# Two-layer diffusion backbone on one core: the first FFN in three parts instead of two, more chunks of the second FFN by the block product, and own buffers for a pair of attention's output projection

## What is computed

```python
def swiglu(h, w_in, w_out):
    gate, up = jnp.split(h @ w_in, 2, axis=-1)          # D_FF = 2816 = 22 chunks of 128
    return (jax.nn.silu(gate) * up) @ w_out

def ffn_half_step(xs, md, k, g, w_in, w_out):
    h = modulate(xs, g, md[3 * k], md[3 * k + 1])
    return xs + 0.5 * md[3 * k + 2] * swiglu(h, w_in, w_out)

mod_l = silu(c) @ ada_w[i] + ada_b[i]                   # 9 vectors of 1024 per layer
mod_c = silu(c_ctx) @ ada_w[i] + ada_b[i]
xl = ffn(xl); xl = xl + mod_l[5] * mixer(xl, xc); xl = ffn(xl)     # the same for xc, but for the last layer's end
```

## Time and profile before

| | us |
|---|---|
| median of 3 runs | 2492.06 (2489.99 to 2493.7) |
| the profiled execution, its own time | 2490.07 |
| its span | 2488.3 |
| PE busy | 2443.8 (98% of the span) |
| DVE, ACT, POOL busy | 1652.9, 916.8, 435.7 |

### The profile page before, as it was taken

The page is one execution under the profiler, slowest core; times in us unless marked ns, Lnnn a source line. Parts: engine busy times, 40 slices in busy tenths (PEclk is TensorE's granted clock), DMA queues, the critical chain, the costliest instruction groups (busy, mean ns, idle before and its releaser), DMA issues.

```text
span 2488.3 us, 40985 instructions
## 1 busy us (share of the span) xinstructions
PE 2443.8 (98%) x14665; PEld 2183.7 (88%) x14665; DVE 1652.9 (66%) x2610; ACT 916.8 (37%) x1455; POOL 435.7 (18%) x530
## 2 busy tenths in 40 slices
PE   8999999999999999999999999999999999999999
PEld 7888888888888888999899999999899988888887
DVE  6888678864888857757684747485877775643332
ACT  4333223332633322424441424243555563331221
POOL 0111111212211111000200000002666762000000
PEclk9999999999999999999999999999999999999999
DMA  7545444541155542222212222223111112433332
GB/s 237 164 144 164 131 135 139 156 120 41 46 158 155 155 129 79 66 68 63 73 52 72 72 59 84 61 68 94 26 51 44 32 34 68 127 99 95 93 107 87
DMA packets 367438, 239.51 MB, mean 96 GB/s; under 512 B 8081, under 2 KB 366066, under 8 KB 367346
## 3 DMA queue, kind: packets, MB, share of 16 engines
q1 hardware_dynamic: 366896, 238.12, 33.0%
q10 hardware_dynamic: 450, 0.18, 0.0%
HBM read 236.18 MB, written 2.10 MB: 96 GB/s over the span
## 4 chain that ended last, share of the span: by engine, by line
PE 77%; issue 13%; DVE 5%; POOL 3%; ACT 2%; DMA 0%; POOLq 0%; ACTq 0%; SPq 0%; DVEq 0%
PE pu L1495 46%; PE pu L1692 15%; PE pv L1882 5%; PE pu L1900 1%; PE pu L1537 1%; POOL ada_acc L859 1%; DVE xn L2489 1%; DVE h_lo L2496 1%; PE pu L1919 1%; PE pv L1910 1%; PE pu L1562 1%; PE pv L1789 1%; PE pv L1537 1%; PE pv L1613 0%; DVE w_lo L2138 0%
## 5 line engine op out<-in xcount | busy, mean ns | idle before, releaser
L1495 PE MATMUL pu<-h_hi,w_hi 128*128 128x512 f32 (+1 forms) x1536 | 443.9, 351 | 1.6 <-DVE w_lo L2138 1.0
L1495 PE MATMUL pu<-h_lo,w_hi 128*128 128x512 f32 (+1 forms) x1536 | 442.6, 350 | 0.0
L1495 PE MATMUL pu<-h_hi,w_lo 128*128 128x512 f32 (+1 forms) x1536 | 441.0, 349 | 0.0
L2138 DVE TENSOR_TENSOR w_lo<-w_raw,w_hi 128x1024 fp32r<-128x1024 f32 (+3 forms) x208 | 277.6, 1337 | 173.3 <-ACT w_hi L937 166.8
L937 ACT ACTIVATE w_hi<-w_raw 128x1024 fp32r<-128x1024 f32 (+3 forms) x208 | 221.0, 1063 | 443.2 <-PE pu L1495 406.9
L2165 DVE SCALAR_TENSOR_TENSOR ada_acc<-ada_raw,cs,ada_acc 128x384 f32<-128x384 f32 x602 | 345.2, 615 | 11.2 <-DVE ada_acc L2165 2.0
L1495 PEld LDWEIGHTS pu<-h_hi,w_hi 128*128 128x128 f32 x1536 | 246.7, 188 | 42.8 <-DVE w_lo L2138 2.0
L1495 PEld LDWEIGHTS pu<-h_hi,w_lo 128*128 128x128 f32 x1536 | 248.1, 188 | 40.5
L859 POOL TENSOR_TENSOR ada_acc<-ada_acc,ada_parts 128x768 f32<-128x768 f32 x86 | 147.5, 1716 | 770.2 <-ACT ada_parts L944 715.4
L1495 PEld LDWEIGHTS pu<-h_lo,w_hi 128*128 128x128 f32 x1536 | 247.2, 188 | 38.8
L2389 DVE SCALAR_TENSOR_TENSOR xT<-pu,gate,xT 128x512 f32 (+3 forms) x142 | 84.3, 630 | 289.5 <-PE pu L1495 286.3
(11 more groups left out here) (313 smaller groups left out, 4989.7 us busy)
## 6 DMA issues: line engine op xcount, KB each, us to landing
ada_raw<-in_ada_w SPq DMA_DIRECT2D x86, 768.0 KB, 4.7
w_raw<-in_ffn_w_in SPq DMA_DIRECT2D x116, 512.0 KB, 3.9
w_raw<-in_ffn_w_out SPq DMA_DIRECT2D x40, 704.0 KB, 4.5
w_raw<-in_ffn_w_in SPq DMA_DIRECT2D x108, 256.0 KB, 3.0
w_raw<-in_diff_w_qkv SPq DMA_DIRECT2D x21, 512.0 KB, 5.2
w_raw<-in_ffn_w_out SPq DMA_DIRECT2D x24, 384.0 KB, 3.3
first_raw<-in_ada_w SPq DMA_DIRECT2D x8, 1024.0 KB, 10.5
w_raw<-in_ffn_w_out SPq DMA_DIRECT2D x24, 320.0 KB, 3.3
```

The source lines that it names most:

```text
L1495: last = pe.matmul(banks(ch, s_), w[:, j, :], r[:, SEG[s_]], start=(j == 0 and i == 0), stop=(j == k - 1 and i == 2))
L2138: dve.tensor_tensor(w_lo[:, ch, 0:k * P], w_raw[:, ch, 0:k * P], w_hi[:, ch, 0:k * P].bitcast(F32), ALU.subtract).then_inc(split_ready[ch], 1)
```

## The change

**FFN 0** runs in parts of 8, 7 and 7 chunks instead of 11 and 11. It has the same matmuls of in and out units, four more out pairs (34 pairs instead of 30), and out units with K = 8 or 7 instead of 11; its tail has K = 7. **Granules:** four of layer 1 move from FFN 1 to FFN 0: `ADA_L1` is (11, 11, 0, 2), so that pairs 1 to 30 of FFN 0 and 1 to 11 of FFN 1 have a granule (before: 1 to 26, and 1 to 15). **FFN 1** runs one plain part of 7 chunks instead of 11, and then block parts; four more chunks go by the block product, in a block part of their own with K = 4 out pairs. **First block chunk:** ACT makes the SiLU and the held copy of product P5 ahead of the hi copies for the next chunk. **Attention's output:** the second pair has its own slots (a half in the upper third of `w_raw`, `w_hi`, `w_lo`; the other half in `second_raw`, `w_again`, `second_rest`, which lie over memory that the heads have left) and its own banks, and PE works on it between the steps of the last head. The core of the diff:

```diff
-PART_PAIRS = FP + OUT_PAIRS
-FFN_PAIRS = PARTS * PART_PAIRS
+FFN_PARTS = {0: ((0, 8), (8, 7), (15, 7)), 1: ((0, 7),), 3: ((0, FP), (FP, FP))}
+FFN_PAIRS = {k: sum(kp + OUT_PAIRS for _, kp in parts) for k, parts in FFN_PARTS.items()}
...
-BLK_PARTS = {1: ((11, 6, 3, 0), (17, 5, 0, 3)),
+BLK_PARTS = {1: ((7, 6, 3, 0), (13, 4, 0, 3), (17, 5, 0, 7)),
...
-ADA_L1 = (7, 15, 0, 2)
+ADA_L1 = (11, 11, 0, 2)
...
+            for ch in range(2):
+                load_unit(ch, PAIR_WO, wslot(w_raw, ch, DC), wo[:, :, ch, :])
+            sp.wait_ge(tq_done, 3 * HEADS)
+            sp.wait_ge(ss_ready, TT * HEADS)
+            for ch in range(2):
+                for b, dst in enumerate((w_raw[:, ch, DC * P:], second_raw[:, ch, :])):
+                    sp.dma_start(dst.rearrange("p (k c) -> p k c", k=DC // 2),
+                                 wo[:, b * DC // 2:(b + 1) * DC // 2, 2 + ch, :]).then_inc(second_in[ch], 16)
...
-                if nxt is None:
+                if sums:
                     block_w_hi(g + 1, P1)
+                    block_silu(g, 0)
+                    block_hold(g, 1, pu[:, 2], P5)
                     block_w_hi(g + 1, P6)
+                    block_w_hi(g + 1, P2)
...
-                k, x_hi, x_lo = FP, a_hi, a_lo
+                k, x_hi, x_lo = FFN_PARTS[0][-1][1], a_hi, a_lo
...
-            out_chunk(HEADS - 2, (0,))
+            second_out(0)
             out_sums(HEADS - 1)
+            second_out(1)
             out_spread(HEADS - 1)
-            out_chunk(HEADS - 1, (0,))
-            for j in (HEADS - 2, HEADS - 1):
-                out_chunk(j, (1,))
+            second_out(2)
+            second_out(3)
             for ch in range(2):
-                unit(ch, PAIR_WO + 1, DC, lambda j: h_hi[:, j], lambda j: h_lo[:, j], NL)
+                for j in (HEADS - 2, HEADS - 1):
+                    out_chunk(j, (ch,))
+            for j in range(4, DC):
+                second_out(j)
             wide_pe(5)
```

More of the change, by code:

```diff
@@ L93, with parts_of @@
 SUM_LAG = 2
+def parts_of(k):
+    return [(q, f0, kp, f0 + OUT_PAIRS * q, k not in BLKS and f0 + kp == FC) for q, (f0, kp) in enumerate(FFN_PARTS[k])]
 def beside(k, pair, lag=1):
@@ L140, in build @@
         KMAX = 12
+        again = ExitStack()
+        w_again = sb("w_again", [P, 2, KMAX * P], F32R, again)
+        again.close()
         w_raw = sb("w_raw", [P, 2, KMAX * P])
@@ L246, in build @@
         attn.close()
+        second = ExitStack()
+        second_skip = sb("second_skip", [P, SECOND_SKIP], F32, second)
+        second_raw = sb("second_raw", [P, 2, DC // 2 * P], F32, second)
+        second.close()
+        rest = ExitStack()
+        rest_skip = sb("rest_skip", [P, SECOND_SKIP], F32, rest)
+        second_rest = sb("second_rest", [P, 2, DC // 2 * P], F32R, rest)
+        rest.close()
         wo_late = ExitStack()
@@ L398, in build @@
         next_in = [sem(f"next_in{i}") for i in range(2)]
+        second_in = [sem(f"second_in{i}") for i in range(2)]
+        second_hi = sem("second_hi")
+        second_split = sem("second_split")
         head_in = sem("head_in")
@@ L1108, in ffn_act @@
                     else:
-                        out_pair(OUT_PAIRS - 1, nxt if last else DC, [beside(k, p0 + PART_PAIRS - 1, lag) for lag in (1, SUM_LAG)])
+                        out_pair(OUT_PAIRS - 1, nxt if last else DC, [beside(k, p0 + kp + OUT_PAIRS - 1, lag) for lag in (1, SUM_LAG)])
+                if k in BLKS:
+                    block_act(k)
             def block_w_hi(g, p, free=None):
@@ L1358, in out_hi, with second_w_out @@
                 act.activation(h_hi[:, g, 0:NL], oT[:, g, :], ACT.Copy).then_inc(onh_ready, 1)
+            def second_w_out(b):
+                for ch in range(2):
+                    act.wait_ge(second_in[ch], 32)
+                    if b == 0:
+                        act.wait_ge(qkv_done, TT * HEADS)
+                    else:
+                        act.wait_ge(second_split, 2)
+                    act.activation(second_w(ch, b)[1], second_w(ch, b)[0], ACT.Copy).then_inc(second_hi, 1)
+                    if b:
+                        act.sem_inc(raw_ready[ch], 16)
             def attn_act(h, do_a, do_b, do_c):
@@ L1476, in _ @@
             out_hi(HEADS - 1)
-            for ch in range(2):
-                split_hi(ch, PAIR_WO + 1, DC)
+            second_w_out(1)
             square_out(5, PAIR_WO, 0)
@@ L1630, in ffn_pe @@
                 n = FFN_N[k]
-                for q in range(PARTS):
-                    if k in BLKS and q:
-                        block_pe(k)
-                        break
-                    b = PAIR_FFN[k] + q * PART_PAIRS
+                for q, f0, kp, p0, ends in parts_of(k):
+                    b = PAIR_FFN[k] + p0
                     first = 0
@@ L1643, in ffn_pe @@
                         first = 1
-                    for lo, hi, ada in spans(k, q * PART_PAIRS, first, FP, SUM_LAG):
+                    for lo, hi, ada in spans(k, p0, first, kp, SUM_LAG):
                         with pe.Fori(lo, hi) as f:
@@ L1965, in out_chunk, with second_out @@
                         last.then_inc(unit_done[ch], 1)
+            def second_out(j):
+                if j == 0:
+                    pe.wait_ge(second_split, 2)
+                if j == DC // 2:
+                    for ch in range(2):
+                        pe.wait_ge(split_ready[ch], PAIR_WO + 3)
+                pe.wait_ge(on_split, j + 1)
+                for ch in range(2):
+                    hi, lo = (t[:, j % (DC // 2) * P:(j % (DC // 2) + 1) * P] for t in second_w(ch, j // (DC // 2))[1:])
+                    for i, (w, x_) in enumerate(((hi, h_hi), (hi, h_lo), (lo, h_hi))):
+                        last = pe.matmul(second_bank(ch, 0), w, x_[:, j, 0:NL], start=(j == 0 and i == 0), stop=(j == DC - 1 and i == 2))
+                    if j == DC - 1:
+                        last.then_inc(unit_done[ch], 1)
             def attn_pe(h, do_b, do_a, do_c, ahead=0):
```

193 lines of the change are left out of this document (108 added, 85 removed).

## The result

The changed kernel takes 2525.76 us (median of 4 runs, 2522.51 to 2527.8) where the kernel before takes 2491.73 in runs beside it: a ratio of 1.0138, 95% interval 1.0125 to 1.0151. It is slower by 34 us. The forecast was 15 us slower, 2505, and the range ended at 2518. The profiled execution took 2522.51 with a span of 2520.7, 32.4 more than the span before, 2488.3.

What follows compares the result with a forecast made beforehand. PE bounds the kernel, 77% of the chain that ended last. Terms -9.8 + 21.5 + 6.1 - 6.2 - 0.4 + 4 = +15.2 us on 2490 gave 2505 us; forecast's own range 2498 to 2511, full range 2488 to 2518.

Steps and rivals of the forecast that it cites:

- The clock: Falls of PE's granted clock behind five new waits near 3 us and one near 5.6: +4 us, bounds 0 and 10.
- the clock falls behind every long wait: Rival, chance 0.15: each of five waits and the tail brings a stretch at 0.50, +6 to +10 more, 2511 to 2516.
- The granule's chain: Out pairs of FFN 0 and 1 with granules, too short for the granule's steps across engines: +21.5 us, bounds 0 and +27.
- The tail: FFN 0's end with K = 7: PE waits 5.6 us ahead of the sums, not 0.75; +6.1 us, bounds +4 and +8.
- K = 4: FFN 1's new block part with short out pairs, channel 1's addition behind six DVE instructions: 0 us, bound 1.
- Attention's output: Second output pair worked on between the last head's steps: 16.3 us instead of 22.5, -6.2 us, bounds -7.0 and -3.
- Block chunks: Four more chunks by the block product, 14.56 us each instead of 17.0 for a whole pair: -9.8 us.
- Held copy: Copy made sooner in the first block chunk, twice in the kernel: -0.2 us each, -0.4; bound -1.2 each.

Runs made afterwards that it cites:

- fill: The changed kernel plus 207 matmuls whose result nobody reads, put where PE waits in FFN 0, its tail and FFN 1: 2508.63 us, ratio 1.0071.

## Why the prediction was wrong in size

Direction, places and releasers were right; two terms and a bound were too small.

- **The clock is the step that failed**: "I take half of them: +4, with bounds 0 and 10". The clock fell at all seven waits over 2 us beside granules and in the tail, and `fill` prices this at 14.2 us, past the bound. The reasoning took a gap of 0.98 us with no fall as evidence on waits of 3 to 5.6. And it read that "this trace has it once, at rows 11", which is wrong: the kernel before is at 0.50 in four more stretches before its end, from about 654, 1774, 2043 and 2122 us, 20 us together, and the last three stand behind waits of only 1.0 to 1.8 us. Windows around two of them:

```profile
2043.00:2048.00 5.00, 4.91 (x24) 3.63 (x22) 4.20 (x10) 3.27 (x7) 1.78 (x2) 0.66 0.00 0
2121.00:2131.00 10.00, 9.39 (x48) 8.57 (x48) 7.60 (x15) 6.48 (x10) 0.00 (x0) 0.66 0.33 93
```

  These rows spoke for the rival "the clock falls behind every long wait", and it was the case that happened. By the section "HAM oscillation — how this bites in real kernels" of the Trainium skill's page "TensorE: Matmul & The Clock Gate", cited with that rival, the loss is paid at each tile anew; the runs agree, with seven falls at seven waits.
- **The granule's chain** (+21.5). `fill` leaves 72.9, 70.4, 35.4 and 70.1 us against 69.6, 61.6, 30.8 and 61.6 unhindered, so 25.2; the forecast starts gave 73.4, 68.8, 34.1 and 68.8. So K = 8 came out 0.5 us shorter than forecast and the rest 4.2 longer. The recurrence holds (with K = 7 `fill` has starts 20.0, 15.4, 19.6 and 15.4 apart), and the link that was mis-sized is the last: "at its end DVE now meets POOL's subtraction, so I take 18.7". That collision was named and priced at 0.3; the split took 2.33 instead of 1.0 us, and the first distance was 20.1. Another 0.3 of the difference lies between the split's end (400.79) and PE's start (401.10), which the sum left out. For K = 8 it took 18.6 where its own rule, with a split of 1.61 x 8/11, gives 18.8; that slip is small.
- **The tail** (+6.1): the wait is 5.5 against 5.6, and with the clock kept up by the filler the tail takes the forecast's 25.5 us. Its further 3.4 are the clock's. The term took DVE's list whole, 9.85 us, and didn't name the 2.5 us in it in which DVE waits for POOL; it came out right because DVE meets POOL at the same operations in both kernels.
- **K = 4** (0, bound 1): 2.1. By DVE's timeline (1132.89 to 1139.93) two of the six instructions ahead of channel 1's addition waited 0.9 and 0.2 us for weights that had just landed, and one waited 0.7 for ACT's hi copy. The bound did not count these.
- **Attention's output** (-6.2): -7.0, at a granted clock of 1.00 all through; in the last head before it 1 us is lost, where a stretch at 0.50 stands (2095.7 to 2099.1) behind waits of only 1.1 us each. Why the clock fell there was not tried. **Block chunks** (-9.8): as forecast, 14.56 us each. **Held copy** (-0.4): not above 0.3, as argued from DVE's order.

With the measured terms put in place of the forecast ones the sum is 15.2 + 10.2 (clock) + 3.7 (chain) + 2.1 (K = 4) - 0.8 + 1.0 (attention) + 0.1 (held copy) = 31.5, against 32.4 in the spans. The range failed because clock and chain are not independent: a longer chain makes a longer wait, and each wait buys its stretch at half speed. The rival's 2516 with the chain's upper bound on top, +5.5, makes 2521.5. It was in the prediction's own numbers, close to the 2522.5 of the profiled execution, and past the end of the range.

## What to carry to other kernels

A wait in front of PE can have a second price, the stretch at half clock that comes with it. Go through the granted clock of the whole trace before you call a fall the only one. Where a long wait has such a fall, take it for every wait of that kind, and test it with filler matmuls, which need little other change. Before work is put beside a shorter stage, walk the chain through each engine's order for several rounds, and price every link at what it takes beside its new neighbour. And take a change with several parts apart: here one part was worth -6 us and was buried under another of +40.
